# Differential attention: the second probability tile scaled on ACT and added on POOL instead of one VectorE operation

## The chip, the cores and the metric

The kernel runs on one core of one Trainium2 chip. The metric is the device time of one execution in microseconds (us), the median of several runs. The engines are TensorE (PE in the profile, its weight loads PEld), VectorE (DVE), ScalarE (ACT), GpSimd (POOL) and SyncE (SP, which issues most of the transfers).

## What is computed

The reference is one step of a two-layer backbone: in each layer a token mixer of three groups of heads (neighbourhood attention, DeltaNet, differential attention) and a channel mixer, for 128 context tokens and 512 latent tokens, 1024 wide. The change lies in differential attention (6 heads of 64, each with two sets of queries and keys of 32):

```python
def diff_attend(qi, k, v, lam):
    s = jnp.einsum('bqhid,bkhid->bhiqk', qi, k, preferred_element_type=jnp.float32) * DF_QK ** -0.5
    p = jax.nn.softmax(s, axis=-1)
    a = (p[:, :, 0] - lam * p[:, :, 1]).astype(v.dtype)
    return jnp.einsum('bhqk,bkhd->bqhd', a, v)
```

So two softmax matrices are made for the same queries, and the second, times a learnt scalar, is taken from the first before the product with the values.

## The kernel before

The kernel is written engine by engine: each engine has its own program, in a fixed order, and semaphores tie them together. In each of the two layers a stage does the attention of both kinds after the DeltaNet stage and before the output projection.

The stage is a list of 60 jobs (`jobs`): five tiles of 128 queries (tile 0 is the context, "prompt"), and in each tile six neighbourhood heads ("na") and then six differential heads ("df"). A prompt job has 128 keys, any other 640. A neighbourhood job has one score matrix (an "item"), a differential job two. Jobs run in two segments, the 12 prompt jobs and the other 48, as a software pipeline of about three jobs in flight:

- TensorE, for each j: `mix_values(j - 1)` (turned probabilities times values, ten instructions for a large job), `turn_probs(j)` (the 128x640 probabilities are transposed in five blocks, ten instructions, lines 1001 to 1015; the fifth block goes to a bank that `outputs(j - 1)` has to have read first, line 1011), `scores(j + 2)`.
- VectorE, for each j: `outputs(j - 1)` (line 1948, scales the result by one over the row sum), `move_last(j)` (line 1941, copies the fifth turned block; it waits for the end of `turn_probs(j)`), `combine(j + 1)` (lines 1917 to 1933), `maxima(j + 2)` (row maxima, line 1914, and their negated, scaled value, line 1915).
- ACT, for each j: `move_probs(j)` (line 1426, copies the four other turned blocks), `exps(j + 2)` (line 1418, the exponentials with row sums, one or two of 128x640).
- POOL has nothing to do in this stage. Its program comes from the DeltaNet stage and goes on with line 2207, the low halves of the output projection's weights, which wait for ACT's line 1440.

In `combine` a neighbourhood job needs one reciprocal (line 1925) and no change to the probabilities. A differential job waits for both exponentials, then computes three one-column operations (lines 1929 to 1931): the factor `cc` = lam x sum0 / sum1 (lam is held negated, so a sum gives the difference) and `rc` = 1 / sum0. Line 1932 then writes prob0 + cc x prob1 over prob0, 128x640 or 128x128, and raises `v_p`, for which line 1004 of `turn_probs` waits. Probability tiles lie in six slots (`prob`, SLOTS).

Of the kernel before, what the change touches and what calls it, by code (L numbers as in the profile page):

```python
# [26 lines left out]
ALU = mybir.AluOpType  # L27
ACT = mybir.ActivationFunctionType
# [5 lines left out]
P = 128  # L34
# [3 lines left out]
TOK = TILES * P  # L38
# [78 lines left out]
JOBS = TILES * (H_NA + H_DF)  # L117
SLOTS = 6
# [61 lines left out]
def build(nc, x_in, cond_in, ada_bias_in, const_in, par_in, ln_in, ada_in, feat_in, tokm_in, out_in,  # L180
          unit_in, down_in, moe_gu_in, moe_down_in, zero_in, ctx_na_k, ctx_na_v, ctx_df_k, ctx_df_v, state_in, rpb_in,
          y_prompt, y_sample, new_na_k, new_na_v, new_df_k, new_df_v, new_state):
    with ExitStack() as ctx:
# [84 lines left out]
        def r32(ap):  # L268
# [26 lines left out]
        prob = [bP[:, s * TOK:(s + 1) * TOK] for s in range(SLOTS)]  # L295
# [3 lines left out]
        gct, alog, mx, nb, sm, rc, cc, lamw, lam, st6, mv, rstd, subw, ssq, lampr, wts = parts(  # L299
            misc[:, 400:], 80, 8, SLOTS, SLOTS, SLOTS, 4, 4, 2, 1, 12, 10, 5, HD, 50, DFQ, 15)  # L300
# [26 lines left out]
        def sem(name):  # L327
            return ctx.enter_context(nc.semaphore(name))
# [84 lines left out]
        a_dn = [sem(f"act_dn{d}") for d in range(2)]  # L413
        a_exp = sem("act_exp")
        a_pt = sem("act_probs_moved")
        a_ot = sem("act_outputs_high")
        a_oh = sem("act_out_weights_high")
        a_gb = sem("act_gate_rows")
# [27 lines left out]
        v_p = sem("vec_probs")  # L446
# [21 lines left out]
        g_xg = sem("pool_sum_gated")  # L468
        g_lo = sem("pool_weights_low")
        g_st = sem("pool_state_zero")  # L470


        def units_before(l):
# [85 lines left out]
        jobs = [(t, kind, h) for t in range(TILES) for kind in ("na", "df") for h in range(6)]  # L559
        first_item, n_items = [], 0  # L560
# [5 lines left out]
            return max(n for n in range(JOBS) if first_item[n] <= it)  # L566

        biased_before = [sum(j[1] == "na" and j[0] > 0 for j in jobs[:n]) for n in range(len(jobs) + 1)]
        five_before = [sum(j[0] > 0 for j in jobs[:n]) for n in range(len(jobs) + 1)]
        N_BIASED, N_FIVE = biased_before[-1], five_before[-1]  # L570
        PROMPT_JOBS = H_NA + H_DF
# [143 lines left out]
        def _(pe):  # L715
# [4 lines left out]
            for l in range(DEPTH):  # L720
# [51 lines left out]
                for i in range(FEAT_TILES):  # L772
                    n = i // 2
# [10 lines left out]
                    hi, lo = (r32(w).rearrange("p (i k f) -> p i k f", i=2, k=KD) for w in (proj_hi[n % 2], slot[fixed_slot(FIRST_FEAT + n)]))  # L784
# [14 lines left out]
                for n in range(25):  # L799
                    c, t = n // TILES, n % TILES  # L800
# [10 lines left out]
                    hi, lo = (r32(w).rearrange("p (k f) -> p k f", k=KD) for w in both)  # L811
# [51 lines left out]
                for n, tiles in enumerate(dn_units):  # L863
                    vb, ab, gb = (c * (UNITS_DN * l + n) for c in (DN_V, DN_A, DN_G))
                    for d in range(2):
                        t, b = tiles[d], 4 * d
# [19 lines left out]
                    if n < UNITS_DN - 1:  # L886

                        i = ADA_FIRST + ADA_EARLY + 2 * n
# [72 lines left out]
                for kc in range(GRID_W):  # L961
                    g, j = kc // 5, kc % 5
# [38 lines left out]
                def turn_probs(j):  # L1001
                    t, kind, h = jobs[j]
                    pr = prob[first_item[j] % SLOTS]
                    pe.wait_ge(v_p, JOBS * l + j + 1)
                    if j >= 1:

                        pe.wait_ge(a_pt, JOBS * l + j)
                    for s in range(1 if t == 0 else TILES):
                        if s == 4:

                            pe.wait_ge(v_o, JOBS * l + j)
                        dst = bank(6, s * P, (s + 1) * P) if s < 4 else bank(7, 0, P)

                        mm = pe.matmul(dst, pr[:, s * P:(s + 1) * P], ident, start=True, stop=True)  # L1014
                    mm.then_inc(s_pt, 1)
# [30 lines left out]
                for t in range(TILES):  # L1046
                    pe.wait_ge(v_fin, TILES * l + t + 1)
                    for g in range(2):
                        n = 2 * t + g
# [22 lines left out]
                for n in range(20):  # L1072
                    c, t = n // TILES, n % TILES
# [5 lines left out]
                    hi, lo = (r32(w).rearrange("p (k f) -> p k f", k=KD) for w in (proj_hi[c % 2], slot[fixed_slot(FIRST_OUT + c)]))  # L1079
# [174 lines left out]
        def _(act):  # L1254
# [3 lines left out]
            for l in range(DEPTH):  # L1258
# [141 lines left out]
                def exps(j):  # L1400
                    t, kind, h = jobs[j]
                    for i in range(1 if kind == "na" else 2):
                        it = first_item[j] + i
                        b, s = 2 * (it % 3), it % SLOTS
                        act.wait_ge(v_nb, n_items * l + it + 1)
                        if it >= SLOTS:

                            act.wait_ge(s_pt, JOBS * l + job_of(it - SLOTS) + 1)
                        scale = HD ** -0.5 if kind == "na" else DFQ ** -0.5
                        if t == 0:  # L1410
                            src, dst = bank(b, 0, P), prob[s][:, 0:P]
                        elif kind == "na":
                            src = dst = prob[s]
                            scale = 1.0
                        else:
                            src = psum[:, b * BANK:(b + 2) * BANK].rearrange("p (g t) -> p g t", g=2)[:, :, 0:HALF]
                            dst = prob[s].rearrange("p (g t) -> p g t", g=2)
                        act.activation(dst, src, ACT.Exp, bias=nb[:, s:s + 1], scale=scale,
                                       accum_out=sm[:, s:s + 1]).then_inc(a_exp, 1)

                def move_probs(j):
                    w = P if jobs[j][0] == 0 else 4 * P
                    act.wait_ge(s_pt, JOBS * l + j + 1)
                    if j >= 2:
                        act.wait_ge(s_pv, JOBS * l + j - 1)
                    act.copy(probT[j % 2][:, 0:w], bank(6, 0, w)).then_inc(a_pt, 1)  # L1426

                for lo, hi in SEGMENTS:
                    exps(lo)
                    exps(lo + 1)  # L1430
                    for j in range(lo, hi):
                        move_probs(j)
                        if j + 2 < hi:
                            exps(j + 2)

# [132 lines left out]
        def _(v):  # L1568
# [107 lines left out]
            for l in range(DEPTH):  # L1676
# [240 lines left out]
                def combine(j):  # L1917
                    t, kind, h = jobs[j]
                    it = first_item[j]
                    s0, s1 = it % SLOTS, (it + 1) % SLOTS  # L1920
                    w = P if t == 0 else TOK
                    c = j % 4
                    if kind == "na":
                        v.wait_ge(a_exp, n_items * l + it + 1)
                        v.reciprocal(rc[:, c:c + 1], sm[:, s0:s0 + 1]).then_inc(v_p, 1)
                        return

                    v.wait_ge(a_exp, n_items * l + it + 2)
                    link(v.reciprocal(cc[:, c:c + 1], sm[:, s1:s1 + 1]))
                    link(v.scalar_tensor_tensor(cc[:, c:c + 1], cc[:, c:c + 1], sm[:, s0:s0 + 1], lam, ALU.mult, ALU.mult))  # L1930
                    link(v.reciprocal(rc[:, c:c + 1], sm[:, s0:s0 + 1]))
                    v.scalar_tensor_tensor(prob[s0][:, 0:w], prob[s1][:, 0:w], cc[:, c:c + 1], prob[s0][:, 0:w],
                                           ALU.mult, ALU.add).then_inc(v_p, 1)

                def move_last(j):
                    if jobs[j][0] == 0:
# [174 lines left out]
        def _(pool):  # L2111
# [34 lines left out]
            for l in range(DEPTH):  # L2146
# [8 lines left out]
                for r in range(6):  # L2155
                    i = 12 + r
# [12 lines left out]
                for n, tiles in enumerate(dn_units):  # L2169
# [26 lines left out]
                    for m in range(1, NLEV):  # L2196
                        for d in range(2):
# [3 lines left out]
                                pool.wait_ge(g_dn[d], gb + 6)  # L2201
                            masked(d, m).then_inc(g_dn[d], 1)

                for c in range(OUT_LOADS):
                    pool.wait_ge(a_oh, OUT_LOADS * l + c + 1)
                    w = slot[fixed_slot(FIRST_OUT + c)]
                    pool.tensor_tensor(r32(w), w, high(proj_hi[c % 2]), ALU.subtract).then_inc(g_ol, 1)
# [117 lines left out]
```

## Time and profile before

| what | us |
|---|---|
| median of 3 runs (3660.49 to 3689.18) | 3661.13 |
| the profiled execution | 3654.36 |
| its span in the trace | 3652.6 |
| attention stage of layer 0, in the trace | about 690 to 928 |
| attention stage of layer 1, in the trace | about 2210 to 2445 |

Over the span TensorE is busy for 3187.3 us (87%), VectorE for 1922.4 (53%), ACT for 1288.7 (35%), POOL for 462.0 (13%). These are averages over stages with different limits; the stage in question has to be read by itself. A row of the timeline gives start and duration in us, engine, line, operation, output and inputs with their shapes (partitions x elements); in square brackets stands how long the engine was idle before it, and which instruction ended that. "PEclk" is the share of full TensorE clock that was granted: 1.00 is 2.4 GHz, 0.50 is 1.2 GHz.

### The profile page before, as it was taken

The page shows a single profiled execution, that of the slowest core. Times are in us where ns is not written, and L with a number is a line of the kernel's source. Part 1 is how long each engine was busy: PE and PEld are TensorE (multiplying, and loading weights), DVE is VectorE, ACT ScalarE, POOL GpSimd, SP SyncE. Part 2 cuts the span into 40 slices and gives each one's busy share as a digit, 9 for nine tenths or more (in the row PEclk, how much of TensorE's full clock was granted, in tenths as well). Part 3 has the DMA queues.
Part 4 walks back from the last instruction along what each step waited for, and adds up shares of the span by engine and source line. Part 5 has one row for each costly group of instructions (what it writes and reads, how often), then busy time and mean ns, then how long its engine had stood idle before and what let it go on. Part 6 is the DMA issues. An engine that isn't in the chain of part 4 may idle for free.

```text
span 3652.6 us, 50853 instructions
## 1 busy us (share of the span) xinstructions
PE 3187.3 (87%) x20980; PEld 2799.6 (77%) x20980; DVE 1922.4 (53%) x2967; ACT 1288.7 (35%) x1883; POOL 462.0 (13%) x443
## 2 busy tenths in 40 slices
PE   7997998899779999899979988978689898898892
PEld 5993888777679899689757886758588888788782
DVE  2214444577742222422424445776577777777776
ACT  2114111144222122121141113431466666666662
POOL 0000535000210000100024420001100000000002
PEclk9987999699889999999879986988899999999996
DMA  5243100000011122231210100002588888888783
GB/s 184 81 157 110 47 24 25 22 1 1 12 70 70 64 93 67 89 128 70 102 68 31 41 2 21 1 1 84 200 325 310 321 323 317 325 309 324 292 318 148
DMA packets 76356, 472.91 MB, mean 129 GB/s; under 512 B 10064, under 2 KB 13904, under 8 KB 26960
## 3 DMA queue, kind: packets, MB, share of 16 engines
q1 hardware_dynamic: 52512, 312.36, 23.3%
q0 software_dynamic: 23616, 157.30, 11.8%
q8 instruction: 169, 2.77, 0.3%
q14 instruction: 59, 0.48, 0.0%
HBM read 451.01 MB, written 27.53 MB: 131 GB/s over the span
## 4 chain that ended last, share of the span: by engine, by line
PE 68%; DVE 17%; issue 4%; ACT 4%; POOL 4%; DMA 3%; SPq 0%; ACTq 0%; DVEq 0%; POOLq 0%
PE psum L1222 11%; PE psum L1121 9%; PE psum L791 7%; PE psum L1242 5%; PE psum L814 4%; PE psum L1151 4%; PE psum L906 3%; DVE ring_rounded L1584 3%; PE psum L1082 3%; PE psum L919 3%; PE psum L1014 3%; PE psum L732 3%; DVE arena L1914 3%; PE psum L916 3%; PE psum L1029 2%
## 5 line engine op out<-in xcount | busy, mean ns | idle before, releaser
L1222 PE MATMUL psum<-stage_rounded 128*128 128x256 f32 x3488 | 584.5, 291 | 59.8 <-DVE ring_rounded L1584 38.0
L1222 PEld LDWEIGHTS psum<-stage_rounded 128*128 128x128 f32 x3488 | 511.6, 195 | 81.9 <-DVE ring_rounded L1584 51.9
L1584 DVE TENSOR_TENSOR ring_rounded<-ring,stage_rounded 128x2048 fp32r<-128x2048 f32 (+1 forms) x193 | 425.2, 2217 | 6.5 <-ACT stage_rounded L1515 6.5
L1515 ACT CAST stage_rounded<-ring 128x2048 fp32r<-128x2048 f32 (+1 forms) x193 | 358.5, 1859 | 157.2 <-DMA ring<-in_moe_gu 76.0
L1242 PE MATMUL psum<-stage_rounded 128*128 128x512 f32 x874 | 267.1, 412 | 33.1 <-DVE ring_rounded L1584 20.0
L1222 PE MATMUL psum<-ring_rounded,stage_rounded 128*128 128x256 f32 x1000 | 287.2, 287 | 0.0
L1242 PEld LDWEIGHTS psum<-stage_rounded 128*128 128x128 f32 x874 | 168.9, 195 | 81.2 <-DVE ring_rounded L1584 29.6
L1584 DVE TENSOR_TENSOR stage_rounded<-stage,stage_rounded 128x2048 fp32r<-128x2048 f32 (+1 forms) x96 | 213.0, 2227 | 4.1 <-ACT stage_rounded L1515 4.1
L1515 ACT CAST stage_rounded<-stage 128x2048 fp32r<-128x2048 f32 (+1 forms) x96 | 179.3, 1868 | 82.6 <-PE psum L1242 34.3
L1014 PE MATMUL psum<-arena,stage 128*128 128x128 f32 x1008 | 174.7, 305 | 34.9 <-DVE input L1948 20.0
L732 PE MATMUL psum<-ring,arena 128*2 128x256 f32 x768 | 174.7, 384 | 25.8 <-DMA ring<-in_ada 15.7
L1222 PEld LDWEIGHTS psum<-ring_rounded,stage_rounded 128*128 128x128 f32 x1000 | 196.2, 196 | 0.4
L2189 POOL TENSOR_TENSOR stage<-stage 128x512 f32<-128x512 f32 x140 | 175.4, 1269 | 133.9 <-PE psum L906 133.6
L1014 PEld LDWEIGHTS psum<-arena,stage 128*128 128x128 f32 x1008 | 138.1, 203 | 58.0 <-DVE input L1948 38.8
L1029 PEld LDWEIGHTS psum<-stage 128*128 128x128 f32 x1008 | 128.4, 199 | 67.1 <-ACT stage L1426 40.8
L1121 PE MATMUL psum<-stage_rounded 128*128 128x320 f32 x704 | 161.6, 311 | 12.0 <-POOL ring_rounded L2220 12.0
L1390 ACT COPY stage<-psum 128x512 f32<-128x512 f32 x100 | 58.6, 586 | 293.6 <-PE psum L919 293.6
L1121 PE MATMUL psum<-input_rounded,stage_rounded 128*128 128x320 f32 x704 | 161.4, 310 | 0.0
L1121 PE MATMUL psum<-stage_rounded,ring_rounded 128*128 128x320 f32 x704 | 161.1, 310 | 0.0
L1661 DVE TENSOR_TENSOR stage<-stage,psum 128x128 f32<-128x128 f32 x187 | 53.7, 287 | 202.2 <-ACT stage L1552 201.9
L732 PEld LDWEIGHTS psum<-ring,arena 128*2 128x2 f32 x768 | 63.0, 85 | 124.0 <-ACT arena L1282 14.6
L1029 PE MATMUL psum<-stage 128*128 128x64 f32 x1008 | 146.2, 291 | 4.8 <-ACT stage L1426 4.8
(303 smaller groups left out, 6650.3 us busy)
## 6 DMA issues: line engine op xcount, KB each, us to landing
ring<-in_moe_gu SPq DMA_DIRECT2D x63, 1024.0 KB, 6.3
ring<-in_moe_gu POOLq DMA_DIRECT2D x62, 1024.0 KB, 6.8
ring<-in_ada SPq DMA_DIRECT2D x48, 1024.0 KB, 4.8
stage<-in_moe_gu SPq DMA_DIRECT2D x31, 1024.0 KB, 6.4
stage<-in_moe_gu POOLq DMA_DIRECT2D x31, 1024.0 KB, 6.2
ring<-in_moe_down SPq DMA_DIRECT2D x28, 1024.0 KB, 6.5
ring<-in_moe_down POOLq DMA_DIRECT2D x28, 1024.0 KB, 5.7
ring<-in_unit SPq DMA_DIRECT2D x22, 1024.0 KB, 4.8
```

Source lines behind the costliest of these rows:

```text
L732: mm = pe.matmul(bank(banks[i % 2], 0, 256)[0:2], scond[:, 2 * k:2 * k + 2], w[:, k, :], start=(k == 0), stop=(k == KD - 1))
L791: mm = pe.matmul(bank(b + g, 0, HALF), w[:, i % 2, k, :], r32(x[:, k, g * HALF:(g + 1) * HALF]), start=(k == 0 and m == 0), stop=(k == KD ...
L814: mm = pe.matmul(bank(b, 0, 256 if c < 4 else 16), r32(x[:, k, t * P:(t + 1) * P]), w[:, k, :], start=(k == 0 and m == 0), stop=(k == KD - ...
L1014: mm = pe.matmul(dst, pr[:, s * P:(s + 1) * P], ident, start=True, stop=True)
L1029: mm = pe.matmul(bank(7, 256, 256 + HD), probT[j % 2][:, s * P:(s + 1) * P], VT[:, s, v_at:v_at + HD], start=(s == 0), stop=(s == n - 1))
L1121: mm = pe.matmul(bank(b + 2 * i + g, 0, HALF), w[:, i, k, :], r32(x[:, k, g * HALF:(g + 1) * HALF]), start=(k == 0 and n == 0), stop=(k == ...
L1151: mm = pe.matmul(bank(b), r32(x[:, f, cols]), w[:, j, :], start=(f == 0 and m == 0), stop=(f == UF - 1 and m == 2))
L1222: mm = pe.matmul(bank(h % 2, 0, 2 * P), r32(x[:, cols]), w[:, k, :], start=(k == 0 and m == 0), stop=(k == KD - 1 and m == 2))
L1242: mm = pe.matmul(bank(4 + g), r32(x[:, f, :]), w[:, at], start=(f == 0 and m == 0), stop=(f == UF - 1 and m == 2))
L1515: act.copy(r32(M_HIGH[q % M_HI][:, 0:n]), M_SLOT[q % M_SLOTS][:, 0:n]).then_inc(a_mhi, 1)
L1584: v.tensor_tensor(r32(w), w, high(M_HIGH[q % M_HI][:, 0:n]), ALU.subtract).then_inc(v_mlo, 1)
L2189: return pool.tensor_tensor(AS[:, d], A[:, d], lev[:, d, m].unsqueeze(1).broadcast_to([P, 4, P]), ALU.mult)
```

## The change

Line 1932 goes. `v_p` is raised by the last of the three small operations. ACT, after copying the turned blocks of job j, waits for `v_p` of job j + 1 and scales its second probability tile in place by `cc` (`scale_second`), ahead of the exponentials of job j + 2. POOL waits for ACT and adds the second tile to the first. TensorE's turn of a differential job waits for POOL (`g_p`); that of a neighbourhood job still waits for `v_p`. Prompt jobs are changed too. The diff, with the semaphores' declarations and the two counts (`diff_before`, `N_DIFF`) left out:

```diff
@@ -1001,7 +1005,10 @@
                 def turn_probs(j):
                     t, kind, h = jobs[j]
                     pr = prob[first_item[j] % SLOTS]
-                    pe.wait_ge(v_p, JOBS * l + j + 1)
+                    if kind == "na":
+                        pe.wait_ge(v_p, JOBS * l + j + 1)
+                    else:
+                        pe.wait_ge(g_p, N_DIFF * l + diff_before[j + 1])
                     if j >= 1:
 
                         pe.wait_ge(a_pt, JOBS * l + j)
...
@@ -1425,11 +1432,21 @@
                         act.wait_ge(s_pv, JOBS * l + j - 1)
                     act.copy(probT[j % 2][:, 0:w], bank(6, 0, w)).then_inc(a_pt, 1)
 
+                def scale_second(j):
+                    if jobs[j][1] == "na":
+                        return
+                    s1, w = (first_item[j] + 1) % SLOTS, P if jobs[j][0] == 0 else TOK
+                    act.wait_ge(v_p, JOBS * l + j + 1)
+                    act.activation(prob[s1][:, 0:w], prob[s1][:, 0:w], ACT.Copy, scale=cc[:, j % 4:j % 4 + 1]).then_inc(a_sc, 1)
+
                 for lo, hi in SEGMENTS:
                     exps(lo)
                     exps(lo + 1)
+                    scale_second(lo)
                     for j in range(lo, hi):
                         move_probs(j)
+                        if j + 1 < hi:
+                            scale_second(j + 1)
                         if j + 2 < hi:
                             exps(j + 2)
 
...
@@ -1918,7 +1935,6 @@
                     t, kind, h = jobs[j]
                     it = first_item[j]
                     s0, s1 = it % SLOTS, (it + 1) % SLOTS
-                    w = P if t == 0 else TOK
                     c = j % 4
                     if kind == "na":
                         v.wait_ge(a_exp, n_items * l + it + 1)
...
@@ -1928,9 +1944,7 @@
                     v.wait_ge(a_exp, n_items * l + it + 2)
                     link(v.reciprocal(cc[:, c:c + 1], sm[:, s1:s1 + 1]))
                     link(v.scalar_tensor_tensor(cc[:, c:c + 1], cc[:, c:c + 1], sm[:, s0:s0 + 1], lam, ALU.mult, ALU.mult))
-                    link(v.reciprocal(rc[:, c:c + 1], sm[:, s0:s0 + 1]))
-                    v.scalar_tensor_tensor(prob[s0][:, 0:w], prob[s1][:, 0:w], cc[:, c:c + 1], prob[s0][:, 0:w],
-                                           ALU.mult, ALU.add).then_inc(v_p, 1)
+                    v.reciprocal(rc[:, c:c + 1], sm[:, s0:s0 + 1]).then_inc(v_p, 1)
 
                 def move_last(j):
                     if jobs[j][0] == 0:
...
@@ -2201,6 +2215,12 @@
                                 pool.wait_ge(g_dn[d], gb + 6)
                             masked(d, m).then_inc(g_dn[d], 1)
 
+                for j in range(JOBS):
+                    if jobs[j][1] == "df":
+                        w = P if jobs[j][0] == 0 else TOK
+                        s0, s1 = (prob[(first_item[j] + i) % SLOTS][:, 0:w] for i in range(2))
+                        pool.wait_ge(a_sc, N_DIFF * l + diff_before[j + 1])
+                        pool.tensor_tensor(s0, s0, s1, ALU.add).then_inc(g_p, 1)
                 for c in range(OUT_LOADS):
                     pool.wait_ge(a_oh, OUT_LOADS * l + c + 1)
                     w = slot[fixed_slot(FIRST_OUT + c)]
```

## Rows read from the trace of the kernel before

**Rows 1.** by stretches (busy per engine, granted clock, DMA, GB/s)

```profile
core 0: us, PE busy (x) PEld busy (x) DVE busy (x) ACT busy (x) POOL busy (x), PEclk, DMA share, GB/s
760.00:770.00 10.00, 9.12 (x68) 7.30 (x67) 8.46 (x23) 5.11 (x11) 0.00 (x0) 1.00 0.01 2
780.00:790.00 10.00, 9.94 (x62) 7.15 (x61) 6.08 (x17) 2.90 (x7) 0.00 (x0) 1.00 0.01 2
```

**Rows 2.** one line's instructions (ns, shortest/median/longest): line 1932

```profile
L1932 DVE SCALAR_TENSOR_TENSOR stage<-stage,arena x60: 351/884/886, 703.2 to 2438.9; 128x640 f32<-128x640 f32 x48, 128x128 f32<-128x128 f32 x12
```

**Rows 3.** order of time, one differential job (start, us, engine, line, operation)

```profile
757.87 0.29 DVE L1941 COPY stage<-psum 128x128 f32<-128x128 f32 x1 [0.58 <-PE psum L1014]
...
758.52 0.16 DVE L1931 RECIPROCAL arena<-arena 128x1 f32<-128x1 f32 x1
758.72 0.89 DVE L1932 SCALAR_TENSOR_TENSOR stage<-stage,arena 128x640 f32<-128x640 f32 x1
...
759.52 0.82 DVE L1914 TENSOR_REDUCE arena<-psum 128x1 f32<-128x640 f32 x1
...
760.21 1.11 PE L1014 MATMUL psum<-arena,stage 128*128 128x128 f32 x8
...
761.42 0.28 DVE L1948 TENSOR_SCALAR input<-psum,arena 128x64 f32<-128x64 f32 x1
...
761.76 0.49 PE L1014 MATMUL psum<-arena,stage 128*128 128x128 f32 x2 [0.44 <-DVE input L1948]
...
762.28 0.29 DVE L1941 COPY stage<-psum 128x128 f32<-128x128 f32 x1 [0.58 <-PE psum L1014]
```

**Rows 4.** order of time, ends of two groups of six differential jobs

```profile
749.03 0.29 DVE L1941 COPY stage<-psum 128x128 f32<-128x128 f32 x1 [0.58 <-PE psum L1014]
...
775.48 0.29 DVE L1941 COPY stage<-psum 128x128 f32<-128x128 f32 x1 [0.58 <-PE psum L1014]
...
900.50 0.29 DVE L1941 COPY stage<-psum 128x128 f32<-128x128 f32 x1 [0.58 <-PE psum L1014]
...
924.40 1.35 PE L1014 MATMUL psum<-arena,stage 128*128 128x128 f32 x10
...
925.79 0.29 DVE L1941 COPY stage<-psum 128x128 f32<-128x128 f32 x1 [0.90 <-PE psum L1014]
```

**Rows 5.** groups by line and shape, ACT (busy us, mean ns | idle)

```profile
L1418 ACT ACTIVATE stage<-stage,arena 128x640 f32<-128x640 f32 x48 | 39.7, 828 | 132.0 <-DVE arena L1915 132.0
...
L1296 ACT CAST stage_rounded<-input 128x640 fp32r<-128x640 f32 x24 | 16.9, 726 | 14.3 <-DVE input L1687 13.9
...
L1418 ACT ACTIVATE stage<-psum,arena 128x128 f32<-128x128 f32 x36 | 13.2, 368 | 25.2 <-DVE arena L1915 25.2
```

**Rows 6.** instructions of a line (ns, shortest/median/longest): POOL lines 2189, 2183, 2225

```profile
L2189 POOL TENSOR_TENSOR stage<-stage x140: 1257/1269/1281, 370.8 to 2157.5; 128x512 f32<-128x512 f32 x140
...
L2183 POOL TENSOR_TENSOR arena<-stage,arena x20: 615/616/619, 368.5 to 2123.0; 128x256 f32<-128x256 f32 x20
...
L2225 POOL TENSOR_TENSOR stage<-stage,arena x5: 1997/2975/2979, 1519.2 to 1529.0; 128x1024 f32<-128x1024 f32 x5
```

**Rows 7.** order of time, hand-overs from ACT to POOL and from POOL to PE

```profile
365.57 0.63 ACT L1380 ACTIVATE stage<-stage 128x512 f32<-128x512 f32 x1
...
366.27 1.04 POOL L2177 TENSOR_TENSOR stage<-stage,arena 128x512 f32<-128x512 f32 x1 [2.60 <-ACT stage L1380]
...
373.36 1.27 POOL L2189 TENSOR_TENSOR stage<-stage 128x512 f32<-128x512 f32 x1
...
374.68 0.50 PEld L898 LDWEIGHTS psum<-arena,stage 128*128 128x128 f32 x2 [0.95 <-POOL stage L2189]
```

**Rows 8.** order of time, a VectorE operation beside one of POOL

```profile
929.76 4.50 POOL L2207 TENSOR_TENSOR ring_rounded<-ring,stage_rounded 128x2048 fp32r<-128x2048 f32 x1 [286.51 <-ACT stage_rounded L1440]
...
929.82 5.12 DVE L1958 TENSOR_TENSOR stage<-input 128x640 f32<-128x640 f32 x1
```

**Rows 9.** the trace by stretches, in the DeltaNet stage

```profile
435.00:440.00 5.00, 3.52 (x28) 3.14 (x28) 1.58 (x3) 0.00 (x0) 4.93 (x5) 1.00 0.64 269
```

More of the change, by code:

```diff
@@ L415, in build @@
         a_pt = sem("act_probs_moved")
+        a_sc = sem("act_second_scaled")
         a_ot = sem("act_outputs_high")
@@ L470, in build @@
         g_st = sem("pool_state_zero")
+        g_p = sem("pool_probs")
         def units_before(l):
@@ L568, in build @@
         biased_before = [sum(j[1] == "na" and j[0] > 0 for j in jobs[:n]) for n in range(len(jobs) + 1)]
+        diff_before = [sum(j[1] == "df" for j in jobs[:n]) for n in range(len(jobs) + 1)]
+        N_DIFF = diff_before[-1]
         five_before = [sum(j[0] > 0 for j in jobs[:n]) for n in range(len(jobs) + 1)]
```

## The prediction, made before the changed kernel was run

> **What bounds the kernel now.** I read the stretches first, then the timeline of one job, then single lines. The change touches only the attention stage of each layer, so the question is what sets the pace of one differential job there. In a stretch of such jobs TensorE is busy 9.12 of 10 us at the full granted clock (1.00, the 2.4 GHz level), VectorE 8.46, ACT 5.11 and POOL not at all; in a stretch of neighbourhood jobs TensorE is at 9.94 and VectorE at 6.08 [rows 1]. So the neighbourhood jobs are TensorE's, and nothing there changes. The differential jobs are closer to VectorE's, and the timeline shows how [rows 3]: line 1941 of one job starts at 757.87 and that of the next at 762.28, a period of 4.41 us. In it VectorE runs without a gap except for the 0.58 that line 1941 waits for TensorE, and TensorE waits only 0.44 us, in the middle of a turn, for line 1948 (its fifth tile needs the output bank to be read). VectorE, in its written order, reaches line 1948 late because line 1932 (0.89 us) stands ahead of the row maxima. That is the operation that the change removes.
>
> The reader is to see two things that pull against each other. VectorE's work sets the period today. But VectorE computes job j+1's probabilities only after line 1941 of job j, and that waits for the end of job j's turn. So "end of turn j, combine j+1, turn j+1" is a closed loop, with slack today and of a length that the change alters.
>
> The sums that follow use the ends of whole groups. Six large differential jobs take from 749.03 to 775.48, 26.45 us; the last group of a layer takes from 900.50 to 925.79, 25.29 us, because its last turn has no score products ahead of it [rows 4]. There are 48 large jobs and 12 small (prompt) ones in the two layers [rows 2], so eight groups, two of them last ones. Layer 1 shows the same intervals.
>
> **The change, part by part.** Removed: 48 operations of 0.884 us and 12 of 0.351 us on VectorE [rows 2], together 46.6 us of its time. That is not the gain, since it lies in a loop with others.
>
> Added: one ACT operation and one POOL operation for each job, in series, with two more hand-overs. I follow the new loop from the end of a turn (T). Today T is 761.76 + 0.49 = 762.25, or 757.84 one period earlier; line 1931 ends at 758.68 [rows 3], so the semaphore for the scalars now comes at T + 0.84.
>
> - Hand-over to ACT: 0.06, as from line 1948 (ends 761.70) to TensorE (761.76) [rows 3].
> - Scaling on ACT, 128x640 in place, scale from a column: nearest is line 1418's form from SBUF with a column operand, 0.828 us; the cast of 128x640 without one takes 0.726 [rows 5]. I take 0.83, lower bound 0.73. ACT is free at that time: by its order only the 128x512 copy of the turned tile, which is released at T, stands ahead, and the exponentials come behind.
> - Hand-over to POOL: line 1380 ends at 366.20, POOL starts at 366.27, so 0.07 [rows 7].
> - Addition on POOL, 128x640, two SBUF operands: 0.616 us at 256 columns, 1.269 at 512, so 2.55 ns a column, and 1.269 + 128 x 2.55 ns = 1.60 us. The 1024-column line ran from 1.997 to 2.979 us, in proportion 1.25 and 1.86 us at 640 [rows 6]: these are my bounds.
> - Hand-over to TensorE: POOL ends at 374.63, the weight load starts at 374.68, so 0.05 [rows 7].
> - The turn itself, ten pieces without a wait inside: 1.35 us [rows 4]. The wait inside it goes: line 1948 no longer stands behind line 1932.
>
> The loop is 0.84 + 0.06 + 0.83 + 0.07 + 1.60 + 0.05 + 1.35 = 4.80 us, against 4.41. TensorE itself would be ready to start the turn at 760.21 - 757.84 = T + 2.37 [rows 3], and the operand comes at T + 3.45, so TensorE stands 1.08 us for POOL in each job. What waits behind it: the score products of job j+2 and the values of job j, both later in TensorE's order; VectorE and ACT then wait for those.
>
> One group of six becomes 28.80 us, 2.35 more than 26.45; a last group 3.51 more than 25.29. Six times 2.35 and twice 3.51 make 21.1 us.
>
> The small jobs: off the loop the change would save at most 12 x 0.35 = 4 us. Wholly on it each would lose the scaling (0.37 us, from the 128-column exponential [rows 5]), the addition (0.29 us, the same POOL slope) and the hand-overs (0.18), less 0.41 for line 1932 and its hand-over: 0.43 each, 5 us together. I take 0, with minus 4 and plus 5 as bounds.
>
> What I cost at nothing. POOL's queue is otherwise empty here; its next work, the low halves of the output weights, waits for ACT after the last job anyway. The transfers are not moved. While POOL adds (T + 1.80 to T + 3.40), VectorE does the row maxima and line 1948, whose tensors come from PSUM [rows 3]. This matters because a VectorE operation with both tensors in SBUF that met a POOL operation took 5.12 us, until POOL's 4.50 us were over [rows 8]. If the one-column scaling behind the second maximum were held that way too, it would end near T + 3.5 and line 1948 near T + 3.8; the turn needs that one at about T + 4.4, when eight of its ten pieces are out. That cover of 0.6 us hides it.
>
> The Trainium skill speaks against the move: "GPSIMD Engine Reference", section "Engine selection", puts elementwise work on VectorE and calls GPSIMD about twice as slow on two inputs. Twice 0.884 us would be an addition of 1.77 us and a sum of 29 us in place of 21. The same page's table of 2048 columns (4497 ns), in proportion an estimate of 1.41 us, would give 12 us. The row in hand, 1.27 us at 512 columns [rows 6], lies between the two, and the sum goes by it.
>
> **The rivals.**
>
> *Forecast: the loop becomes the bound.* Plus 21 us. With both low bounds (0.73 and 1.25) the period is 4.35: six times minus 0.35, twice plus 0.81, and minus 4 for the small jobs, so minus 5 us. With 1.86 it is 5.06: six times 3.91, twice 5.07 and 5, so plus 39 us.
>
> *Faster: the leg through ACT and POOL hides behind TensorE.* If scaling, addition and hand-overs fitted into 2.37 - 0.84 = 1.53 us, the period would be TensorE's own, 2.37 + 1.35 = 3.72 us; a group 22.3, so six times minus 4.1 and twice minus 3.0: minus 31 us, about 3630. For it: VectorE does lose 0.89 us of its 4.41. Against it: the leg is 2.61 us by the rows. It decides at an addition of 1.60 - 0.39 = 1.21 us: below that, the change gains. No row has POOL that quick, the contention-free end (1.25) included.
>
> *Much slower: TensorE's clock falls.* TensorE would be busy for about its own 3.72 us of each 4.80. If the clock fell to the 1.2 GHz level, the turn in the loop would take 2.70 us, 1.35 more: 48 x 1.35 = 65 us on top, about 3747. Against it: in the DeltaNet stage the clock stayed at 1.00 in a stretch with 3.52 of 5 us busy and 28 matrix products [rows 9], no denser than the new jobs (28 in 4.8 us).
>
> *The scaling or the addition costs more than any row, or queues.* ACT's busy time rises to about 3.1 of 4.8 us a job, so ACT does not become the bound, and only a slower POOL is left, from about 1.9 us up: above plus 37 us.
>
> **How the numbers follow.** The profiled execution took 3654.4 us (span 3652.6); the median of the runs is 3661.1, and I add the 21 us to that: 3682 us. Forecast 0.83, leg hidden 0.03, clock 0.05, dearer POOL 0.09. The forecast's own range, minus 5 to plus 39, with 1 to 2 us of spread between runs, is 3656 to 3702; that leaves out the other three, 0.17, and needs no widening. About 1% (36.6 us) is what a measurement of this kernel can tell from no change. Above it lie the clock, the dearer POOL and a small tip of the forecast: 0.16. Faster by over 1% needs more than even the hidden leg gives: 0.02. The rest, 0.82, is within 1%.
>
> **What would show it.** Line 1941's period in large differential jobs 4.8 us (right), 4.4 or less (wrong). POOL's new line 1.60 us, ACT's 0.83 us. TensorE's turn waiting about 1.1 us a job for POOL, and no longer for line 1948. VectorE near 3.0 of 4.8 us busy (4.41 less 0.58 and about 0.8). Neighbourhood intervals unchanged at about 4.0 us, clock 1.00. The forecast is wrong if POOL's addition stays below 1.2 us, if VectorE's waits lengthen beyond the cover, or if the clock falls.

## The result, and the profile of the changed kernel

The changed kernel took 3734.15 us (median of 4 runs, 3718.76 to 3756.02), the kernel before 3660.81 us (4 runs, 3649.53 to 3689.18). The ratio is 1.0189, with a 95% interval of 1.0142 to 1.0235: slower by about 69 us. Ratios leave out a run that took over 1.5% more than the fastest of its kernel; in the experiments that is one run of the kernel before and one of the kernel with a longer VectorE operation. 3682 us had been forecast, with 3656 to 3702 as the range. So the sign was right, the size was more than three times too small, and the time lies outside the range.

The loop that was forecast is there. The timeline of one differential job of the changed kernel (start, us, engine, line, operation; line 1955 is the old line 1941, line 1021 the turn, line 1440 the new scaling, line 2223 the new addition):

```profile
767.84 1.38 PE L1021 MATMUL psum<-arena,stage 128*128 128x128 f32 x10 [0.24 <-POOL stage L2223]
...
769.26 0.29 DVE L1955 COPY stage<-psum 128x128 f32<-128x128 f32 x1 [0.70 <-PE psum L1021]
...
769.91 0.16 DVE L1947 RECIPROCAL arena<-arena 128x1 f32<-128x1 f32 x1
770.11 0.83 ACT L1440 ACTIVATE stage<-stage,arena 128x640 f32<-128x640 f32 x1 [0.26 <-DVE arena L1947]
...
771.01 1.53 POOL L2223 TENSOR_TENSOR stage<-stage 128x640 f32<-128x640 f32 x1 [3.23 <-ACT stage L1440]
...
772.60 2.50 PE L1021 MATMUL psum<-arena,stage 128*128 128x128 f32 x10 [0.83 <-POOL stage L2223]
...
775.13 0.29 DVE L1955 COPY stage<-psum 128x128 f32<-128x128 f32 x1 [2.41 <-PE psum L1021]
```

From the end of one turn to the start of the next the chain runs as it was added up: three small operations, ACT 0.83, POOL 1.53, TensorE. The job that ends at 769.26 had begun at 764.50, an interval of 4.76 us where 4.80 was forecast; before it was 4.41 [rows 3]. But look at the two turns. The first takes 1.38 us. The second, the same ten products, takes 2.50, and the next two intervals are 5.87 and 7.01 us. What changed between them is TensorE's clock: it was 1.00 during the first turn and 0.50 during the second. Stretches of the changed kernel (us; busy per engine, then granted clock, DMA share and GB/s; the first is the second turn, the next lies in the first neighbourhood jobs, the other two in differential ones):

```profile
772.60:775.10 2.50, 2.50 (x12) 2.27 (x12) 0.12 (x1) 0.83 (x2) 0.00 (x0) 0.50 0.00 0
750.00:757.00 7.00, 7.00 (x30) 5.54 (x29) 2.56 (x7) 2.35 (x5) 0.00 (x0) 0.50 0.01 2
840.00:847.00 7.00, 5.31 (x36) 4.16 (x36) 4.33 (x14) 4.05 (x8) 2.96 (x2) 1.00 0.01 2
826.00:833.00 7.00, 7.00 (x30) 5.54 (x29) 2.94 (x9) 3.19 (x6) 1.54 (x1) 0.50 0.00 0
```

At 1.00 TensorE is busy 5.31 of 7.00 us and waits for the rest. At 0.50 (the 1.2 GHz level) it is busy all the time, and its own work is what a job takes: 7.0 us. The trace of the kernel before has 1.00 in each of its 48 large differential jobs; [rows 1] has one stretch of them.

The intervals between the ends of the turns, read off line 1941 or 1955, show where that happens (us; the first six columns are neighbourhood jobs, the others differential ones; the first number of a layer's first tile has nothing before it):

```
before, layer 0, first tile      -    6.86 4.00 4.00 4.00 4.04   4.43 4.41 4.41 4.42 4.41 4.37
before, layer 0, second tile     4.00 4.00 4.00 4.00 4.00 4.04   4.42 4.41 4.42 4.41 4.42 4.37
changed, layer 0, first tile     -    7.00 6.99 6.99 7.00 7.00   7.01 4.76 5.87 7.01 4.77 4.76
changed, layer 0, second tile    4.00 4.00 4.00 4.00 4.00 4.05   4.76 5.88 7.01 4.76 4.76 4.76
changed, layer 1, second tile    6.99 4.34 4.00 4.00 4.00 4.04   4.76 4.76 4.75 5.75 4.76 5.89
```

Two things are mixed here: falls of the clock within the differential groups, in every tile, and a start of the first tile at 0.50. Added up over the large jobs of both layers (48 in each, neighbourhood and differential), the profiled execution before has 399.3 us and the changed one 488.1. Of the 88.7 us, the loop at full clock is 6 x 4.76 - 26.45 = 2.1 us for six groups and 3.3 for two, 19 us. The two first neighbourhood groups (35.0 against 22.9 us) are another 24. The five differential jobs right behind them that run on at 0.50 (7.01 us each in place of 4.76) are 11 more, so the slow starts come to 35 and the falls to the other 34. (The whole profiled execution, 3729.93 us, lies 75.6 above that of before; the rest of the kernel took 13 us less in it.)

### The profile page after: what moved, and what is told of

Same layout as the page of the kernel before. It is cut to its first block, busy times and chain, and to the rows that moved or that the text cites. A ratio compares the mean times of both kernels' runs of the same rounds, so it can differ in the third digit from the quotient of the medians.

```text
span 3728.2 us, 50913 instructions
## 1 busy us (share of the span) xinstructions
PE 3256.2 (87%) x20980; PEld 2854.6 (77%) x20980; DVE 1879.4 (50%) x2907; ACT 1340.3 (36%) x1943; POOL 542.2 (15%) x503
## 4 chain that ended last, share of the span: by engine, by line
PE 71%; DVE 13%; POOL 5%; ACT 4%; DMA 3%; issue 3%; SPq 0%; ACTq 0%; DVEq 0%; POOLq 0%
PE psum L1229 10%; PE psum L1128 8%; PE psum L795 7%; PE psum L1249 5%; PE psum L1021 5%; PE psum L818 4%; PE psum L1158 4%; PE psum L910 3%; PE psum L1089 3%; PE psum L923 3%; DVE ring_rounded L1601 3%; PE psum L736 3%; PE psum L1036 3%; PE psum L920 2%; POOL stage L2223 2%
## 5 line engine op out<-in xcount | busy, mean ns | idle before, releaser
L1229 PEld LDWEIGHTS psum<-stage_rounded 128*128 128x128 f32 x3488 | 508.5, 194 | 80.3 <-DVE ring_rounded L1601 49.7
L1021 PE MATMUL psum<-arena,stage 128*128 128x128 f32 x1008 | 197.9, 351 | 47.3 <-POOL stage L2223 33.5
L1249 PEld LDWEIGHTS psum<-stage_rounded 128*128 128x128 f32 x874 | 164.2, 190 | 78.7 <-DVE ring_rounded L1601 30.9
L1021 PEld LDWEIGHTS psum<-arena,stage 128*128 128x128 f32 x1008 | 167.5, 248 | 64.3 <-POOL stage L2223 40.5
L1036 PEld LDWEIGHTS psum<-stage 128*128 128x128 f32 x1008 | 150.7, 229 | 78.4 <-issue 50.4
L1036 PE MATMUL psum<-stage 128*128 128x64 f32 x1008 | 169.6, 323 | 4.1 <-ACT stage L1433 4.1
L2223 POOL TENSOR_TENSOR stage<-stage 128x640 f32<-128x640 f32 (+1 forms) x60 | 79.1, 1319 | 570.0 <-ACT stage L1440 570.0
```

What stands on the lines that cost most here:

```text
L1036: mm = pe.matmul(bank(7, 256, 256 + HD), probT[j % 2][:, s * P:(s + 1) * P], VT[:, s, v_at:v_at + HD], start=(s == 0), stop=(s == n - 1))
L1229: mm = pe.matmul(bank(h % 2, 0, 2 * P), r32(x[:, cols]), w[:, k, :], start=(k == 0 and m == 0), stop=(k == KD - 1 and m == 2))
L1249: mm = pe.matmul(bank(4 + g), r32(x[:, f, :]), w[:, at], start=(f == 0 and m == 0), stop=(f == UF - 1 and m == 2))
L2223: pool.tensor_tensor(s0, s0, s1, ALU.add).then_inc(g_p, 1)
```

## The experiments

The theory after the result, called A in the expectations: the loop costs about 20 us, and the rest is TensorE's clock, which falls because TensorE now stands idle for about 1 us in each differential job. Against it stood B: the low clock has another cause, such as the state in which the large jobs start, or POOL and ACT at work beside TensorE. Ratios are to the kernel before, run on the same chip at the same time, with 95% intervals.

**One group of jobs alone.** First only the 12 prompt jobs were changed, then only the 48 large ones. The edit for the first (the second has the conditions the other way round):

```diff
-                    if kind == "na":
+                    if kind == "na" or t > 0:
                         pe.wait_ge(v_p, JOBS * l + j + 1)
...
-                    if jobs[j][1] == "na":
+                    if jobs[j][1] == "na" or jobs[j][0] > 0:
                         return
...
-                    v.reciprocal(rc[:, c:c + 1], sm[:, s0:s0 + 1]).then_inc(v_p, 1)
+                    if t == 0:
+                        v.reciprocal(rc[:, c:c + 1], sm[:, s0:s0 + 1]).then_inc(v_p, 1)
+                        return
+                    w = P if t == 0 else TOK
+                    link(v.reciprocal(rc[:, c:c + 1], sm[:, s0:s0 + 1]))
+                    v.scalar_tensor_tensor(prob[s0][:, 0:w], prob[s1][:, 0:w], cc[:, c:c + 1], prob[s0][:, 0:w],
+                                           ALU.mult, ALU.add).then_inc(v_p, 1)
```

> Only the 12 prompt jobs are changed; the 48 large differential jobs keep the VectorE operation. Theory A: the large jobs have their 4.41 us at clock 1.00; the kernel is within 5 us of the kernel before (ratio 0.998 to 1.002). Theory B in its likeliest form (the changed prompt jobs shift the start of the large ones, and the first tile stays at 1.2 GHz): the neighbourhood jobs of the first tile take 7.0 us each, which is about 12 us or more per layer, ratio 1.007 or more.

> Only the 48 large differential jobs are changed; the 12 prompt jobs keep the VectorE operation. Theory A: the clock falls in the differential groups as in the changed kernel, intervals of 5.9 and 7.0 us among those of 4.76, ratio 1.012 to 1.02. Theory B (prompt jobs set the state): the intervals are 4.76 us throughout and the ratio is about 1.006.

Prompt jobs alone: 1.0008 (0.9977 to 1.0040), no change. The large ones alone: 1.0108 (1.0024 to 1.0191). So the prompt part costs nothing, as forecast, and the large jobs carry the loss. The second ratio lies a little below the 1.012 to 1.02 of A, and its interval is too wide to tell that range from the 1.006 of B; what tells A from B here is the trace. In the profile of the second, the first tiles start as before (6.89, then 4.00 us), and the falls are there in every tile: 4.76, 4.76, 4.76, 5.74, 4.77, 5.89, then 6.99 for the next neighbourhood job.

The first gave something not expected. In its layer 1, where the large jobs themselves are as before, TensorE stayed at 0.50 through the first neighbourhood jobs and five differential ones, all at 7.0 us. One stretch of it:

```profile
2240.00:2300.00 60.00, 60.00 (x232) 47.50 (x232) 27.52 (x73) 17.23 (x36) 0.00 (x0) 0.50 0.00 1
```

So the slow start of the first tile comes with the old large jobs as well. The prompt jobs ahead of it are the changed ones here, but the kernel with a longer VectorE operation, below, has no part of the change, and its trace starts at 0.50 in both layers (6.99 to 7.01 us between the neighbourhood jobs of the first tile). That part of B is right, and the slow start needs nothing of the change. Whether the change makes it more frequent, these few traces do not show.

**Breaking the loop by order.** On VectorE the small operations of job j+1 were put ahead of the copy of job j's fifth block, and on ACT the scaling ahead of the copy of the other four.

```diff
-                        move_last(j)
                         if j + 1 < hi:
                             combine(j + 1)
+                        move_last(j)
...
-                        move_probs(j)
                         if j + 1 < hi:
                             scale_second(j + 1)
+                        move_probs(j)
```

> The changed kernel with two steps in another order: on VectorE the small operations of job j+1 stand before the copy of job j's fifth block, on ACT the scaling for job j+1 before the copy of job j's other four. So the addition for job j+1 can run while job j is turned, and no loop passes through it. Theory A: TensorE hardly waits for POOL, the interval of the differential jobs is 4.0 to 4.3 us, the clock stays at 1.00, and the kernel takes 5 to 20 us less than the kernel before (ratio 0.994 to 0.999). Theory B: the interval at full clock falls likewise, but stretches at 1.2 GHz stay, and the ratio is 1.005 or more.

Measured: 1.0192 (1.0106 to 1.0277), a miss for A and within what B had named (1.005 or more). But the new order did not do what both had counted on, an interval of 4.0 to 4.3 us: in the first differential group of layer 0 the intervals were 4.04, 4.73, 5.63, 4.73, 5.63 and 4.28 us, the two of 5.63 at a granted clock of 0.70, and whole groups ran at 7.0. The timeline of this kernel shows why:

```profile
754.34 0.83 ACT L1440 ACTIVATE stage<-stage,arena 128x640 f32<-128x640 f32 x1 [0.68 <-DVE arena L1947]
...
755.07 0.56 ACT L1433 COPY stage<-psum 128x512 f32<-128x512 f32 x1
...
755.69 1.91 PE L1036 MATMUL psum<-stage 128*128 128x64 f32 x10 [0.92 <-ACT stage L1433]
```

POOL no longer holds TensorE up, but the copy of the turned blocks (line 1433) now stands behind the scaling on ACT, which waits for VectorE's small operations and through them for the exponentials, and TensorE waits 0.92 us for that copy instead, in about every second job. The loop was moved, not broken. TensorE still has a wait as long as before, and the clock falls just the same, which fits A, but does not tell it from B.

**Filling the wait.** TensorE was given matrix products to do while it waits for POOL: four, then two, of the identity by itself, into the PSUM bank that the turn overwrites.

```diff
                             mix_values(j - 1)
+                        if jobs[j][0] and jobs[j][1] == "df":
+                            for _ in range(4):
+                                pe.matmul(bank(6, 0, P), ident, ident, start=True, stop=True)
                         turn_probs(j)
```

> The changed kernel with four matrix products of the identity by itself, into the PSUM bank that the turn behind them overwrites, put into TensorE's program before each turn of a large differential job, where it waits about 1 us for POOL. Nothing else is changed; the output is the same. Theory A (the loop over ACT and POOL costs about 20 us; what is above that is TensorE's clock, which falls because TensorE stands idle about 1 us in every differential job): once the clock is at 1.00 it stays there in the differential groups, their interval is 4.75 to 4.9 us, no interval of 5.9 or 7.0 follows one at full clock, and the ratio to the kernel before is about 1.005 to 1.010. Theory B (the clock falls in these jobs for another reason, such as POOL and ACT working beside TensorE): intervals of 5.9 and 7.0 stay among those of 4.8, ratio 1.015 or more.

> As the last, with two such products in place of four, so that about half of TensorE's wait stays. Theory A: fewer falls of the clock than in the changed kernel, perhaps none; ratio between 1.005 and 1.015. Theory B: as in the changed kernel, 1.015 or more.

Four: 1.0090 (1.0053 to 1.0127). Two: 1.0097 (1.0058 to 1.0135). Both lie inside the ranges of A and below the 1.015 of B. In the profile with four, once the clock is up, all 46 differential intervals are 4.76 or 4.77; with two, all but one, the very last of layer 0 (5.88). While the clock was still low the products cost time: the first differential job took 8.71 us with four, against 7.01. One job in the timeline of the kernel with two (line 1049 is the filling, line 2226 the addition):

```profile
757.29 1.53 POOL L2226 TENSOR_TENSOR stage<-stage 128x640 f32<-128x640 f32 x1 [3.23 <-ACT stage L1443]
757.88 0.66 PE L1049 MATMUL psum<-arena 128*128 128x128 f32 x4
758.88 1.38 PE L1021 MATMUL psum<-arena,stage 128*128 128x128 f32 x10 [0.34 <-POOL stage L2226]
```

And a stretch of it, with the columns as above:

```profile
750.00:770.00 20.00, 18.64 (x137) 14.96 (x136) 11.65 (x37) 13.10 (x27) 6.13 (x4) 1.00 0.00 1
```

ACT and POOL do exactly what they do in the changed kernel, and TensorE does useless work on top; it has 0.34 us of wait left of 0.83, and the clock holds. So POOL's and ACT's activity does not bring the clock down by itself; the cause lies in what TensorE does in these jobs. The products shorten TensorE's wait and add to its work at once, and no run here tells which of the two holds the clock.

**The wait without the change.** The kernel before got one more VectorE operation ahead of line 1932, so that its interval lengthens without any part of the change.

```diff
                     link(v.reciprocal(rc[:, c:c + 1], sm[:, s0:s0 + 1]))
+                    if t:
+                        v.tensor_tensor(sqo[:, 0:190], TT[:, 0:190], TT[:, 0:190], ALU.mult)
```

> The kernel before, without any part of the change, with one more VectorE operation of 128x190 on unused data ahead of the one that the change removes, in each large differential job. It takes about 0.36 us and should lengthen the interval from 4.41 to about 4.77 us, the interval of the changed kernel, with TensorE waiting about 0.8 us in the middle of the turn; ACT and POOL do what they did. Theory A: the clock falls in the differential groups, intervals of 5.9 and 7.0 appear, ratio 1.010 to 1.02. Theory B: 4.77 throughout at clock 1.00, ratio about 1.005.

Measured: 1.0088 (1.0039 to 1.0137), where A had put 1.010 or more and B about 1.005; the interval holds both. The added operation (line 1933) took 0.36 us. TensorE's wait in the middle of the turn is now 0.71 us, where it was 0.44 [rows 3]:

```profile
828.58 0.49 PE L1014 MATMUL psum<-arena,stage 128*128 128x128 f32 x2 [0.71 <-DVE input L1950]
```

A stretch of the same kernel, within a fall (the 10 us behind it have 0.95):

```profile
936.00:946.00 10.00, 10.00 (x47) 8.50 (x46) 6.64 (x17) 4.12 (x9) 0.00 (x0) 0.54 0.00 1
```

The intervals at full clock are 4.68 or 4.69 us, and 4.99 and 7.01 stand among them, with POOL idle and ACT as before: 48 x 0.28 us is 13 us, and the ratio stands for 32. The profiled execution took 3738.64 us, the longest of six (3682.89 to 3738.64), and the ratio is that of the other five, so the count of falls in it is no measure of the others; that these lost 19 us more than the added operation explains is what fits A here, and with an interval of 14 to 50 us on the 32 it fits, without proving it. The falls in the trace do show that neither the scaling on ACT nor an addition on POOL is needed for one.

**The start of the large jobs.** TensorE got four wide products to do in the 4 us in which it waits for the first large probabilities, in the kernel before and in the changed one.

```diff
                     scores(lo + 1)
+                    if lo:
+                        for _ in range(4):
+                            pe.matmul(bank(6), ident, keep[:, 0:BANK], start=True, stop=True)
```

> The kernel before, with four products of the 128-row identity with 512 columns into an unused stretch of PSUM at the start of the large jobs, where TensorE waits about 4 us for the first probabilities. It asks whether the granted clock can be brought up there. If it can: the first neighbourhood jobs take 4.0 us instead of up to 7.0, and runs in which the clock stays at 0.50 for several jobs do not occur; ratio 0.995 to 1.000. If the start state does not depend on this wait: ratio 0.999 to 1.003, with the same scatter between runs.

> The changed kernel with the four wide products at the start of the large jobs that made the kernel before faster by 0.5% (there the first neighbourhood jobs took 4.0 us). Theory A has three parts: the loop over ACT and POOL (about 19 us), the clock's falls inside the differential groups, and a start at 1.2 GHz that the kernel before has too in some of its runs. Here the third goes: first neighbourhood jobs at 4.0 us, but intervals of 5.9 and 7.0 stay in the differential groups; ratio 1.006 to 1.013. If the falls are only a relic of the start state (theory C), no interval above 4.8 is left and the ratio is 1.000 to 1.003.

The kernel before with it: 0.9948 (0.9925 to 0.9971), 3649.52 us against 3666.72, and the runs lie closer together (3638.43 to 3656.06 against 3651.04 to 3690.79). In the kernel before, the first large turn takes 2.50 us behind a wait of 3.97:

```profile
723.59 2.50 PE L1014 MATMUL psum<-arena,stage 128*128 128x128 f32 x10 [3.97 <-DVE arena L1925]
```

With the edit the four products (line 1039) stand in that wait, and the same turn takes 1.28:

```profile
719.30 5.11 PE L1039 MATMUL psum<-arena 128*128 128x512 f32 x8
...
724.25 1.28 PE L1014 MATMUL psum<-arena,stage 128*128 128x128 f32 x10
```

The stretch from within the products on (the 10 us before it have 0.50):

```profile
722.00:732.00 10.00, 9.97 (x55) 6.80 (x54) 5.14 (x16) 3.18 (x8) 0.00 (x0) 0.99 0.10 40
```

One of the 48 differential intervals of this trace is 4.91 us at a granted clock of 0.73, so a single fall comes with the old wait too.

The changed kernel with it: 1.0153 (1.0101 to 1.0205), above the expectation of 1.006 to 1.013. The first neighbourhood jobs of the changed kernel so started take 4.0 us, and then the differential ones fall, at once: 5.52, 7.01, 7.00, 7.01, 4.76, 5.90. So the falls are no relic of the start. The better start takes 0.52% from the kernel before and 0.36% from the changed one (1.0189 to 1.0153), known to about 0.2 and 0.7%: the slow start is no visible part of what sets the two apart.

**Both together.** The changed kernel with the products at the start and two in each wait:

> The same with two products in TensorE's wait of each large differential job besides. Theory A: all differential intervals 4.76 us at clock 1.00, all neighbourhood ones 4.0; what is left is the loop alone, 6 x 4.76 - 26.45 = 2.1 us a group and 3.3 in the last, 19 us in all, on top of the 0.9948 of the kernel before with the same products at its start: ratio 0.999 to 1.002. If the ratio stays at 1.005 or more, something besides clock and loop costs time.

Measured: 1.0004 (0.9977 to 1.0032), inside the expectation. Every neighbourhood interval is 4.0 and every differential one 4.76, but the last of each layer (5.88). A stretch of it:

```profile
750.00:770.00 20.00, 18.64 (x134) 14.45 (x130) 11.95 (x39) 13.51 (x25) 6.14 (x4) 1.00 0.01 1
```

The account closes. Against the kernel before with the same start (0.9948), the loop alone costs 0.56% or 20 us, as forecast. Against the changed kernel with the same start (1.0153), the clock's falls cost 1.49%, or 55 us. Each ratio has 0.2 to 0.5% of uncertainty, so the first part is known to about 13 us and the second to about 22. The large jobs in the three profiles fit that: 394.3 us, 415.3 with the loop alone, 457.9 with the falls, 42.6 more (in the changed kernel's own trace the falls came to 34).

**A further try for a faster kernel.** Six more such products where TensorE waits for the bias tables, in the kernel before with the better start:

```diff
+                for _ in range(6):
+                    pe.matmul(bank(3), ident, keep[:, 0:BANK], start=True, stop=True)
                 pe.wait_ge(s_bias_in, 32 * (l + 1))
```

> The kernel before with the products at the start of the large jobs, and six more such products into a free PSUM bank where TensorE waits about 4.5 us for the bias tables, ahead of 64 products with 62 rows that take 30 us at 1.2 GHz in each layer. It asks for a version that beats both kernels by more. If those 64 products then run at 2.4 GHz they are bound by VectorE's table additions (0.86 us each, 13 of them) and the stage shortens by up to 15 us a layer: ratio 0.985 to 0.993. If the clock falls again under them: ratio 0.993 to 0.998, as without the six.

Measured: 0.9941 (0.9912 to 0.9970), no different from 0.9948. The six products ran from 652.06 to 657.38, in a stretch at 1.00. The stretch behind them:

```profile
660.00:690.00 30.00, 26.98 (x133) 24.89 (x131) 15.12 (x37) 3.22 (x14) 0.00 (x0) 0.56 0.00 1
```

The clock fell again under the table products that follow. The faster kernel of this study is thus the one before with four products at the start of the large jobs.

## Why the prediction was wrong, step by step

- **What bounds the kernel, and the closed loop**: right. Line 1941's interval went from 4.41 to 4.76 us at full clock; 4.80 was forecast.
- **The terms of the loop**: right, each one. The scaling took 0.83 us (0.83 forecast), the addition 1.533 (1.60), the turn 1.38 (1.35). TensorE's wait for POOL at full clock was 0.84 us a job, not 1.08: the operand came a little earlier, and TensorE's own work takes 3.92 us, where 3.72 had been put. The head of line 2223 (ns of one: shortest, median, longest; then the stretch of the span, and the forms):

```profile
L2223 POOL TENSOR_TENSOR stage<-stage x60: 454/1533/1540, 700.0 to 2528.9; 128x640 f32<-128x640 f32 x48, 128x128 f32<-128x128 f32 x12
```

  The addition at 128 columns took 0.454 us, not the 0.29 of the slope; the prompt jobs had room for it (1.0008). "GPSIMD Engine Reference" of the Trainium skill, section "Engine selection", had said about twice VectorE's time for two inputs; 1.533 against 0.884 us [rows 2] is 1.73 times.
- **The sum of 21 us**: right for what it counted. With the clock held, the loop costs 20 us, known to about 13.
- **Costed at nothing**: right. VectorE's maxima and line 1948 were not held up by POOL (0.154 us for the one-column scaling behind a maximum and 0.283 for line 1948, as before), POOL's next work waited for ACT as before, and the neighbourhood jobs at full clock stayed at 4.00.
- **The rival of the clock**: this is the step that failed, in its chance, in its price and in being left out of the range. It was given 0.05. The evidence against it was a single 5 us stretch of the DeltaNet stage at 1.00 with 3.52 us busy [rows 9], which was taken to speak for 48 jobs in a row with the same wait in each. The trace of before held evidence for it too. The step that rows 9 show comes five times in each layer, the last time behind an idle stretch with the clock already at 0.50. Of the other eight, five held the clock at 1.00 and in three it fell (370 to 380, 490 to 500 and 2005 to 2015 us). One of the three has the same matrix products and, ahead of the fall, the same wait for POOL (0.80 us, where it is 0.81 ahead of rows 9):

```profile
490.00:495.00 5.00, 3.69 (x24) 3.25 (x23) 0.69 (x1) 1.12 (x5) 4.84 (x5) 0.87 0.74 261
495.00:500.00 5.00, 4.20 (x20) 4.06 (x20) 1.61 (x3) 0.00 (x0) 3.58 (x4) 0.50 0.40 162
```

  So the price belonged into the range, and the chance was far too low. In the runs the falls cost about 55 us on top of the loop's 20. The price was wrong in kind: it took 1.35 us on each of 48 jobs for the longer turn. At 0.50 the turn took 2.50 us, but all the rest of TensorE's work was longer too, and a job took TensorE's own 7.0 us; only some of the jobs ran so, and some neighbourhood jobs after a group with them. That 55 lies near the 65 is luck.
- **The runs of before**: 3660.49 to 3689.18 us was read as spread between runs. It may have held a sign, that some executions start their large jobs at 0.50: with four products there the range of ten runs is 18 us wide, against 40 for 16 runs of the kernel before. The trace of that kernel is not of such an execution.
- **Faster, and dearer POOL**: did not happen.

What stays open: why the clock stays at 0.50 through many jobs in some starts and rises after one in others, with the same instructions on TensorE; the runs show that, and that four products change it, not what decides it. Whether the wait or the work missing in it brings the clock down is open too. Of TensorE's wait in a job the runs have few sizes: with 0.34 us (two products) and 0.44 us (the kernel before) the clock held but for single jobs, with 0.71 us (the longer VectorE operation) and 0.84 us (the changed kernel) it fell again and again, and nothing between 0.44 and 0.71 was tried.

## What to carry to other kernels

An operation that is moved to an idle engine lengthens every loop that it lies in; add up the loop from the end of the step that releases it to that same end one round later, and compare it with the work of each engine. If that leaves TensorE with a new wait in every round, price the whole stretch at the lower granted clock as well, as a bound of the range: here the wait itself cost 20 us, and the clock that fell with it about 55. And when a row of the trace speaks against a rival, look at every other place where the same step runs before setting its chance. Whether a slow stretch comes from TensorE's waiting, and not from the other engines, can be tried by giving TensorE harmless products to do in the wait, and where it starts cold behind a wait, the same can be worth keeping.

## What the runs showed of the hardware that was not expected

- TensorE at 0.50 can be busy without a gap for 60 us (60.00 of 60.00 in the stretch above) and stay at 0.50. Four products of 512 columns, 5.11 us long, put ahead of the first large job, were followed by a stretch at 0.99.
- The mean granted clock of a whole execution tracks its time: the changed kernel's four runs have 0.903, 0.899, 0.898 and 0.891 at 3718.76, 3729.93, 3738.37 and 3756.02 us.
- An addition on POOL beside VectorE's work from PSUM took 1.533 us in the median and 1.540 at the longest, and the VectorE operations beside it kept their times (0.283 us for line 1948, as before), where one beside a VectorE operation with both tensors in SBUF held that up by 4.3 us [rows 8] (5.12 us against 0.82 elsewhere).
